# The last layer of a fused two-block network: result-only units on 512 real tokens instead of all 528

## The reference, cut to what matters

```python
h = jnp.concatenate([meta, x], axis=1); h = _layer_norm(h, ln_in_g, ln_in_b)
for l in range(2):
    proj = h @ w_in[l]           # c_val, c_glu, c_gate, q, k, v, a_gate, r_x, r_gate
    c = silu(layer_norm(causal_conv31(c_val * sigmoid(c_glu)))) @ conv_pw_w + conv_pw_b
    y_conv = c * silu(c_gate)
    y_attn = window_attention(rotary(q), rotary(k), v) * silu(a_gate)   # meta keys seen by all
    y_lru = rg_lru(causal_conv4(r_x)) * silu(r_gate)                    # recurrence over tokens
    mixed = concat([y_conv, y_attn, y_lru]) @ w_out[l]
    h = layer_norm(ALPHA * h + mixed)
return h[:, 16:]                 # the meta tokens' own results are dropped
```

## Time and profile before

| what | value |
|---|---|
| median of 3 runs | 3500.57 us (3499.0 to 3501.41) |
| the profiled execution | 3503.06 us, its span 3501.5 us |
| mean granted clock of TensorE | 0.981 |
| PE busy | 3362.5 us, 96% of the span |
| DVE, ACT, POOL busy | 1742.3, 1361.4 and 315.0 us |

### The profile page before, as it was taken

How to read it: one execution, slowest core, us unless ns; L and a number is a source line. 1 busy time by engine, 2 the same in 40 slices (tenths; PEclk the granted TensorE clock), 3 DMA queues, 4 the chain that set the end, 5 groups by cost and what they waited for, 6 DMA issues and landing times.

```text
span 3501.5 us, 58540 instructions
## 1 busy us (share of the span) xinstructions
PE 3362.5 (96%) x21710; PEld 3044.5 (87%) x21710; DVE 1742.3 (50%) x2523; ACT 1361.4 (39%) x2208; POOL 315.0 (9%) x320
## 2 busy tenths in 40 slices
PE   6999999999999999899979999999997999999997
PEld 5888988888888888788869999999996999999996
DVE  5433233344343434424685555556467455555547
ACT  4332233233333333323244444555225445445424
POOL 2000000000000000000000321430000214312000
PEclk9999999999999999999989999999998999999998
DMA  5322233232333232422225222222434222221422
GB/s 184 97 89 86 88 96 96 82 99 82 98 90 90 84 95 78 140 92 91 94 85 158 67 68 69 67 73 74 139 96 146 85 74 68 74 74 58 148 84 85
DMA packets 367751, 327.47 MB, mean 94 GB/s; under 512 B 19712, under 2 KB 363288, under 8 KB 365920
## 3 DMA queue, kind: packets, MB, share of 16 engines
q1 hardware_dynamic: 352064, 291.58, 27.4%
q10 hardware_dynamic: 11136, 19.18, 1.6%
q0 software_dynamic: 4400, 14.62, 1.2%
HBM read 308.23 MB, written 17.07 MB: 93 GB/s over the span
## 4 chain that ended last, share of the span: by engine, by line
PE 38%; issue 12%; DVE 4%; ACT 3%; POOLq 1%; DVEq 1%; POOL 1%; DMA 0%; ACTq 0%
PE ps L513 11%; PE ps L514 11%; PE ps L515 11%; PE ps L853 1%; DVE w_low L1473 1%; PE ps L812 1%; ACT y_layer L1154 1%; DVE residual L1692 1%; ACT x_high L1156 1%; PE ps L827 0%; ACT w_high L979 0%; DVE residual L1707 0%; PE ps L860 0%; PE ps L884 0%; PE ps L831 0%
## 5 line engine op out<-in xcount | busy, mean ns | idle before, releaser
L513 PE MATMUL ps<-x_high,w_high 128*128 128x264 f32 (+3 forms) x5344 | 1753.7, 328 | 74.6 <-DVE w_low L1473 28.7
L514 PE MATMUL ps<-x_low,w_high 128*128 128x264 f32 (+3 forms) x5344 | 1720.2, 322 | 0.0
L515 PE MATMUL ps<-x_high,w_low 128*128 128x264 f32 (+3 forms) x5344 | 1716.4, 321 | 0.0
L1473 DVE TENSOR_TENSOR w_low<-w_raw,w_high 128x1024 fp32r<-128x1024 f32 x544 | 663.5, 1229 | 1086.7 <-ACT w_high L979 1049.9
L513 PEld LDWEIGHTS ps<-x_high,w_high 128*128 128x128 f32 x5344 | 1014.7, 190 | 162.7 <-issue 74.0
L514 PEld LDWEIGHTS ps<-x_low,w_high 128*128 128x128 f32 x5344 | 1015.0, 190 | 81.7 <-issue 3.8
L515 PEld LDWEIGHTS ps<-x_high,w_low 128*128 128x128 f32 x5344 | 1012.3, 189 | 75.5
L979 ACT ACTIVATE w_high<-w_raw 128x1024 fp32r<-128x1024 f32 x544 | 573.2, 1057 | 742.0 <-PE ps L515 607.0
L519 PE MATMUL ps<-w_high,x_high 128*128 128x256 f32 x1184 | 332.3, 281 | 4.7 <-DVE w_low L1473 2.7
L520 PE MATMUL ps<-w_high,x_low 128*128 128x256 f32 x1184 | 332.6, 281 | 0.0
L521 PE MATMUL ps<-w_low,x_high 128*128 128x256 f32 x1184 | 332.6, 281 | 0.0
(11 more groups left out here) (335 smaller groups left out, 2658.9 us busy)
## 6 DMA issues: line engine op xcount, KB each, us to landing
w_raw<-in_w_in SPq DMA_DIRECT2D x792, 256.0 KB, 3.0
w_raw<-in_w_out SPq DMA_DIRECT2D x280, 256.0 KB, 2.9
residual<-residual_stream ACTq DMA_DIRECT2D x8, 1056.0 KB, 11.3
residual_stream<-y_layer ACTq DMA_DIRECT2D x2, 2176.0 KB, 10.1
x_natural<-in_x SPq DMA_DIRECT2D x4, 1024.0 KB, 8.9
x_feature_major<-x_stage POOLq DMA_DIRECT2D x16, 256.0 KB, 4.1
gate_bc<-gate_rows POOLq DMA_DIRECT2D x8, 512.0 KB, 4.4
acc<-x_feature_major POOLq DMA_DIRECT2D x1, 4096.0 KB, 13.5
```

The costliest lines, as they stand in the source:

```text
L513: pe.matmul(dst, wh[:, j, kt, wc], xh[:, k, tok], start=first, stop=False)
L514: pe.matmul(dst, wh[:, j, kt, wc], xl[:, k, tok], start=False, stop=False)
L515: return pe.matmul(dst, wl[:, j, kt, wc], xh[:, k, tok], start=False, stop=last)
L1473: dve.tensor_tensor(wl[:, j], raw[:, j], f(wh[:, j]), ALU.subtract).then_inc(lo_ready, 1)
```

## The change

In the last layer, units whose results reach only the returned tokens run on the 512 real columns: queries, a_gate, r_gate, c_gate, the pointwise product and the output product. Each half of such a unit is one product of 512 columns into one bank (`real=(...)` gives a flag per half). Keys, values, c_val, c_glu and r_x keep 528 columns, and so do the recurrence gates and its scan. The meta queries' own products, copies, masks, reductions and multiply are left out in that layer, with the waits that belonged to them. The steps on DVE, ACT and POOL that follow a 512-column unit also take 512 columns. The final norm's first half has 256 columns in place of 272. POOL's hardware loop over the two layers is written out, since its two layers now differ. The first layer is unchanged.

```diff
+REAL = slice(NM, L)
+REAL_COLS = (slice(NM, H0), slice(H0, L))
...
+        span = lambda n: COLS if n < LAYERS else REAL_COLS
+
+        def shape_of(real):
+            return ((lambda t: t[:, REAL]), (lambda b: ps[:, b, :])) if real else (two, halves)
...
-            with pool.Fori(0, LAYERS) as l:
+            for l in range(LAYERS):
+                real = l + 1 == LAYERS
+                cc = REAL if real else slice(0, L)
...
-                        p = pb[:, i % 2, 0:NM]
-                        pool.tensor_tensor(p, p, small[:, 40:41].broadcast_to([P, NM]), ALU.mult)
+                        if not real:
+                            p = pb[:, i % 2, 0:NM]
+                            pool.tensor_tensor(p, p, small[:, 40:41].broadcast_to([P, NM]), ALU.mult)
...
-                            wj = pl[:, 0, ds(CT * j + g, 1)].broadcast_to([P, L])
+                            wj = pl[:, 0, ds(CT * j + g, 1)].broadcast_to([P, cc.stop - cc.start])
+                            tap = cra[:, j + cc.start:j + cc.stop]
...
-            def unit(U, fill, wide=False, after=(None, None), mid=(None, None), hook=None, tok=slice(0, S)):
+            def unit(U, fill, wide=False, after=(None, None), mid=(None, None), hook=None, tok=slice(0, S), real=(False, False)):
...
+                            if real[m]:
+                                last = three(ps[:, 2 * m, :], k, None, REAL, m, j, kt, k == 0, k == KT - 1)
+                            elif wide:
...
+                c = span(n)[q]
...
+                real = l + 1 == LAYERS
+                parts = (REAL,) if real else (slice(0, LH), slice(LH, L))
...
-                unit(U + O_GRP, fill, wide=True, hook=lambda n: rotate_k() if n == 1 else None)
+                unit(U + O_GRP, fill, wide=True, hook=lambda n: rotate_k() if n == 1 else None, real=(real, real))
...
-                            pe.wait_ge(mo_ready, 2 * G)
-                        for q in range(2):
-                            last = pe.matmul(ps[:, 4 + 2 * t + q, 0:LH], rot[:], qrw[:, t, q * LH:(q + 1) * LH], start=True, stop=True)
+                            if not real:
+                                pe.wait_ge(mo_ready, 2 * G)
+                        for q, c in enumerate(parts):
+                            last = pe.matmul(ps[:, 4 + 2 * t + q, 0:c.stop - c.start], rot[:], qrw[:, t, c], start=True, stop=True)
...
-                        if n == 0:
+                        if n == 0 and not real:
                             last = pe.matmul(ps[:, bank, 160:160 + NM], q[:, 0:BLK], kz[:, i % 2, 0, 0:NM],
                                              start=True, stop=True)
...
-                        if n == 1 and i == 2:
+                        if n == 1 and i == 2 and not real:
                             meta_queries(0)
...
-                        if n == 0:
+                        if n == 0 and not real:
                             last = pe.matmul(ps[:, 6, 3 * BLK:3 * BLK + NM], pb[:, i % 2, 0:BLK], ident[:, 0:NM],
                                              start=True, stop=True)
...
-                        if i == 3:
+                        if i == 3 and not real:
                             meta_queries(1)
...
-                    unit(V + 2, fill, wide=True, hook=behind(16))
-                    unit(V + 3, fill, wide=True, hook=behind(24))
-                    unit(V + 4, fill, wide=True, hook=tail)
+                    unit(V + 2, fill, wide=True, hook=behind(16), real=(real, real))
+                    unit(V + 3, fill, wide=True, hook=behind(24), real=(False, real))
+                    unit(V + 4, fill, wide=True, hook=tail, real=(real, real))
...
-                unit(U + O_CG + 1, fill, wide=True, hook=lambda n: c_var() if n == 0 else None)
+                unit(U + O_CG + 1, fill, wide=True, hook=lambda n: c_var() if n == 0 else None, real=(real, real))
...
+                        for q, tok in enumerate(parts):
+                            dst = ps[:, 2 * t + q, 0:tok.stop - tok.start]
...
-                    unit(U + O_OUT + d, fill + KT, wide=True)
-                finish(l + 1, U + O_OUT + 6, fill + KT, COLS)
+                    unit(U + O_OUT + d, fill + KT, wide=True, real=(real, real))
+                finish(l + 1, U + O_OUT + 6, fill + KT, span(l + 1))
...
-                        p = pb[:, i % 2, 0:NM]
-                        act.activation(p, p, ACT.Exp, bias=small[:, 25:26], accum_out=small[:, 30:31])
-                        act.activation(small[:, 31:36], small[:, 21:26], ACT.Exp,
+                        ns = ST if real else ST + 1
+                        if not real:
+                            p = pb[:, i % 2, 0:NM]
+                            act.activation(p, p, ACT.Exp, bias=small[:, 25:26], accum_out=small[:, 30:31])
+                        act.activation(small[:, 31:31 + ns], small[:, 21:21 + ns], ACT.Exp,
                                        bias=small[:, ds(GROUP * g + i, 1)]).then_inc(att_exp, 1)
...
-                    take(V, 0, two(qrw[:, 0, :]), halves(0))
+                    take(V, 0, cols(qrw[:, 0, :]), banks(0))
...
-                    take(V + 3, 1, two(rgs[:]), halves(2), ACT.Silu)
+                    take(V + 3, 1, cols(rgs[:]), banks(2), ACT.Silu)
...
-                    meta_out(1)
+                    if not real:
+                        meta_out(1)
...
-                            dve.tensor_reduce(small[:, 20:21], pb[:, i % 2, 0:NM], AX.X, ALU.max)
+                            if not real:
+                                dve.tensor_reduce(small[:, 20:21], pb[:, i % 2, 0:NM], AX.X, ALU.max)
                             dve.drain()
-                            dve.tensor_scalar(small[:, 21:26], small[:, 16:21], small[:, ds(GROUP * g + i, 1)], -1.0,
+                            dve.tensor_scalar(small[:, 21:21 + ns], small[:, 16:16 + ns], small[:, ds(GROUP * g + i, 1)], -1.0,
                                               ALU.max, ALU.mult).then_inc(att_max, 1)
 
...
-                        dve.wait_ge(mo_ready, 2 * G + c + 1)
+                        if not real:
+                            dve.wait_ge(mo_ready, 2 * G + c + 1)
                         dve.wait_ge(evac, 2 * (V + 2) + c + 1)
                         y = y2[:, ds(Y_ATT + 2 * g + c, 1), :].squeeze(1)
-                        dve.tensor_tensor(y[:, NM:L], ps[:, 7, :], agt[:, c, NM:L], ALU.mult)
-                        dve.tensor_tensor(y[:, 0:NM], mo[:], agt[:, c, 0:NM], ALU.mult)\
-                           .then_inc(o_taken, 1)
+                        ins = dve.tensor_tensor(y[:, NM:L], ps[:, 7, :], agt[:, c, NM:L], ALU.mult)
+                        if not real:
+                            ins = dve.tensor_tensor(y[:, 0:NM], mo[:], agt[:, c, 0:NM], ALU.mult)
+                        ins.then_inc(o_taken, 1)
...
-                    dve.tensor_tensor(rgx, rth[:], rgs[:], ALU.mult).then_inc(lru_done, 1)
+                    dve.tensor_tensor(rgx[:, cc], rth[:, cc], rgs[:, cc], ALU.mult).then_inc(lru_done, 1)
```

More of the change, by code:

```diff
@@ L1326, in group @@
                     high(V + 1, 2)
-                    take(V, 1, two(qrw[:, 1, :]), halves(2))
+                    take(V, 1, cols(qrw[:, 1, :]), banks(2))
                     high(V + 1, 3)
@@ L1342, in group @@
                     act.wait_ge(c_gated, G + 1)
-                    take(V + 2, 0, two(agt[:, 0, :]), halves(0), ACT.Silu)
+                    take(V + 2, 0, cols(agt[:, 0, :]), banks(0), ACT.Silu)
                     turned(0, 3)
@@ L1351, in group @@
                     turned(1, 2)
-                    take(V + 2, 1, two(agt[:, 1, :]), halves(2), ACT.Silu)
+                    take(V + 2, 1, cols(agt[:, 1, :]), banks(2), ACT.Silu)
                     high(V + 3, 3)
@@ L1389, in _ @@
                 C = U + O_CG
-                take(C, 0, two(cgt[:, 0, :]), halves(0), ACT.Silu)
+                take(C, 0, cols(cgt[:, 0, :]), banks(0), ACT.Silu)
                 for j in range(3):
@@ L1408, in _ @@
                     if j < 3:
-                        fill_piece(j, y2, slice(0, L))
-                take(C + 1, 1, two(cgt[:, 3, :]), halves(2), ACT.Silu)
+                        fill_piece(j, y2[:, :, cc], cc)
+                take(C + 1, 1, cols(cgt[:, 3, :]), banks(2), ACT.Silu)
                 act.wait_ge(c_ready, CT * (l + 1))
```

134 lines of the change are left out of this document (72 added, 62 removed).

## The result

The changed kernel takes 3473.32 us (median; 3472.32 to 3474.90), the kernel before beside it 3500.75 us: ratio 0.9923, 95% interval 0.9908 to 0.9938, 27.4 us less. Forecast were 24.9 us less and 3475.7 us. In a second session it took 3473.83 us against 3498.78 us (ratio 0.9927, 0.9914 to 0.9941), 25.0 us less.

What follows compares the result with a forecast made beforehand. The prediction took the last layer to be bound by PE's issue of products. Its gains less 1.95 us of losses summed to 24.9 us, from a median of 3500.57 us to 3475.7 us, range 3468.5 to 3487 us.

Steps and rivals of the forecast that it cites:

- The forecast case: Last layer: PE's issue of products sets the time, so removed columns are gained; 24.9 us less, 3475.7 us, chance 0.62.
- Part 1: Last layer's units on 512 columns instead of twice 264: 36 halves save 0.48 us each, 17.3 us together.
- Parts 2 and 6: Final product's first half on 256 instead of 272 columns, 1.5 us; final norm's DVE steps on 256 columns, 0.6 us.
- part 3: Narrower pointwise product saves 0.5 us; plain fp32 products (rotations, two sums over convolution features) save 0.4 us.
- Part 4: Meta queries' own score, transpose and value products in the last layer: 40 removed at 0.14 us each, 5.6 us.
- Part 5: Softmax chain ahead of each group's first transpose: chain shortens 0.63 us, PE's wait 0.25 us, 1.0 us for four groups.
- Losses: Gain lost to longer PE waits at group joints, the convolution's variance and the pointwise product: 1.95 us together.
- The joint between groups 0 and 1: PE's 1.52 us wait there, without a releaser, was left as it is, with no gain or loss counted.
- 2: Rival: waits at the attention chains eat the gain in the groups; 13.5 us stay, 3487.1 us, chance 0.17.
- 3: Rival: in the last layer 512 columns cost what twice 264 do; 5 to 7 us stay, about 3494 us, chance 0.05.
- 4: Rival: longer waits at the groups' joints drop PE's clock to 1.2 GHz; 3502 us, up to 3528 us, chance 0.03.
- Rival 1: Chains give more: POOL's multiply worth its 0.88 us, other engines keep up with PE; 3471.0 us, chance 0.12.

Runs made afterwards that it cites:

- e1: Changed kernel with the narrow form kept only in the last layer's output units, last product and final norm: 3492.67 us, ratio 0.9978 to the kernel before.
- e3: Changed kernel with the narrow columns kept but the meta tokens' small products and element work put back: 3483.66 us, ratio 0.9945 to the kernel before.
- e2: Changed kernel with 528 columns back in all units, only the last layer's meta work left out: 3490.59 us, ratio 0.9966 to the kernel before.
- before_again: The kernel before, unchanged, run once more for a second profile: 3499.45 us, ratio 0.9992.

## Why the prediction was right, and where its terms were off

The forecast case came in: the time is PE's issue, and fewer columns come back as time, 27.4 and 25.0 us measured against 24.9. That the numbers lie so near is in part luck, since terms too small by 4.2 us stand against others too large. Its own steps:

- **Part 1, units on 512 columns: right.** 22.24 us between output units; e1 gave the 7.9 us of its parts. In the groups a half gave somewhat less beside scores and transposes: of the 4.5 narrow halves from group 2's first transpose to group 3's rotation 2.16 us were due and, waits set aside, 1.8 us came (87.22 to 85.63 us in e3, whose waits there grew by 0.22 us). The forecast had taken the output units' price over to the groups.
- **Parts 2 and 6: right** as far as e1 tells them. Half units now end 5.68 us apart (3401.95, 3407.63). Of part 6 the 0.3 us behind the first final transposes don't show in the changed kernel (37.5 against 37.4 us). Of part 3 the pointwise product gave its 0.5 us; the plain products weren't measured by themselves.
- **Part 4, meta products: mis-sized.** 0.21 us each, 8.4 instead of 5.6 us. The step that failed is the reading of the earlier trace rows, start of the product to start of the next: it leaves out that the product's two weight loads put off the next product's load.
- **Part 5, the softmax chain: reading right, size off.** The long multiply was contention, and POOL's part is 0.17 us. The wait fell by 0.1 us a group instead of 0.25: e2 took 0.30 away, e3 put 0.21 on. PE came 0.24 + 0.21 = 0.45 us sooner, not 0.38, and the chain shortened by about 0.5 us, not 0.63.
- **Losses:** the wait between groups 1 and 2 is 3.40 us as forecast, the variance's 1.1 us as forecast, the pointwise wait grew by 0.17 us (taken: 0.25). Between groups 2 and 3 only 0.22 us went (0.48 forecast).
- **The joint between groups 0 and 1, left as it is: wrong.** The 1.52 us without releaser were TensorE's loop passage, which a shorter body saves: 1.3 to 1.6 us gained, of which 0.60 us turned into a wait at the rotation.
- **Rivals.** 2 and 3 are refuted by the waits inside the groups (none new) and the spacing. 4 as well: of the three joints between groups only the one of before brought the low level (granted 0.50 from 2975 to 2979 us). Rival 1 came true in a small part, by another road than the one named (meta products and loop passage, not POOL).

From the 24.9 us of the forecast: +2.8 (part 4), +1.4 (passage), -0.6 (part 5), -0.3 (rotation waits) make 28.2 us; 26.6 to 27.9 us were measured in the last layer. What is missing lies mostly in the groups. With the corrected terms the stages from group 0's first transpose to the variance should have gained about 5.3, 4.1, 4.4 and 3.5 us (five halves at 0.48, ten or eight meta products at 0.21, 0.1 each for the softmax wait and the rotation or sums, and the measured changes of the joints' waits); against the first profile of the kernel before, whose slow stretch between groups 1 and 2 is as long as the changed kernel's, they gained 4.8, 4.1, 3.9 and 3.1 us. The half that gives less is 0.35 us in a group of this; why it gives less is open, and so is the rest. Against before_again the same stages gained 14.8 us, as forecast (about 15), with the surplus of part 4 and of the first joint cancelling the half that gives less and the longer slow stretch: the forecast's agreement there is luck.

## What to carry to other kernels

Price a small operation on a bound engine by the neighbours' spacing with and without it, not by its own start to start: its weight loads cost as well. Compare stage by stage and not by the whole layer, since slow stretches move a layer by 1 to 2 us from one execution to the next. A wait of the bound engine without releaser, or with one long done, at a loop's turn is a candidate for instruction fetch; count the instructions of the body and look at whether the instruction queue is silent from the second turn on, since a change that shortens the body may remove it. And a joint can hide two passages behind each other: ScalarE's loop, written out alone, gave 0.9 to 2.2 us, and 6.9 us where TensorE's was gone too.

## What the runs showed of the hardware that was not expected

- TensorE's passage from one turn of a loop to the next cost 1.5 to 2.1 us with 896 or 916 product records in the body (and as many weight loads) and at most 0.3 us with 672 or 652; ScalarE's cost 2.29 us and a table load of 1.28 us, both gone when written out (48 table loads in the last layer instead of 49).
- A product of 16 columns in plain fp32 cost 0.21 us of TensorE's stream, nine tenths of one of 512 columns on split operands (0.2317 us).
- Behind the same wait of 1.91 us the granted clock fell in one execution of the kernel before and stayed at 1.00 in the other, a difference of 1.5 us. A difference of that size between two single profiles tells nothing of the kernels.
